# Expert gate and up weights each as one 4 MB transfer, and the token rows turned by half-identity products

## The reference

```python
lg_exp = ((x2 @ w_re) + b_re).reshape(N, N_GROUPS, EXPERTS_PER_GROUP)     # N = 384 tokens
lg_in = lg_exp[jnp.arange(N), g_sel[:, 0]]
top_v, top_i = lax.top_k(lg_in, TOP_K)                                    # 2 of 8 experts
...
def expert_block(args):                                                   # 32 experts
    xblk, e = args
    return (jax.nn.silu(xblk @ w_eg[e]) * (xblk @ w_eu[e])) @ w_ed[e]     # 2048 -> 512 -> 2048
...
return jax.ops.segment_sum(yb.reshape(n_slots, D) * slot_w[:, None], slot_tok, num_segments=N)
```

## Time and profile before

| | |
|---|---|
| median of three runs | 1981.06 us (1980.61 to 1982.42) |
| the profiled execution | 1982.1 us, of which the span of its instructions is 1980.5 us |
| mean granted TensorE clock | 0.913 of full speed |
| PE busy / PEld busy | 82% / 42% of the span |
| DMA queue of SP | 559.14 MB, 69.5% of 16 engines' span |
| DMA queue of GpSimd | 36.16 MB, 5.4% |

### The profile page before, as it was taken

One profiled execution on the slowest core, in us unless ns is written; L12 is line 12 of the kernel. 1 busy time (PEld: TensorE's weight loads), 2 busy tenths in 40 slices (PEclk: granted clock), 3 DMA queues, 4 the chain that ended last, 5 costly groups with the idle time before them and its releaser, 6 DMA issues.

```text
span 1980.5 us, 21568 instructions
## 1 busy us (share of the span) xinstructions
PE 1622.2 (82%) x8889; PEld 839.3 (42%) x8889; DVE 390.9 (20%) x848; ACT 207.1 (10%) x511; POOL 166.9 (8%) x342
## 2 busy tenths in 40 slices
PE   6899999999986699985888887787878878878850
PEld 2455554444434244444544443444434444444420
DVE  2011212214415100134111111011011110111106
ACT  3001111111122000011000000000000000000003
POOL 1300000000120100002010110110101101001002
PEclk9999999999989799955888989999999889999885
DMA  9986665655560433071799999999999999999953
GB/s 366 338 293 260 229 261 221 261 219 213 212 203 12 170 106 106 31 305 24 319 424 426 428 427 427 427 427 427 425 420 427 423 423 426 424 425 420 422 231 134
DMA packets 100002, 602.26 MB, mean 304 GB/s; under 512 B 15349, under 2 KB 17509, under 8 KB 64745
## 3 DMA queue, kind: packets, MB, share of 16 engines
q1 hardware_dynamic: 83810, 559.14, 69.5%
q0 software_dynamic: 15328, 36.16, 5.4%
q10 hardware_dynamic: 816, 6.29, 0.8%
HBM read 594.65 MB, written 28.10 MB: 314 GB/s over the span
## 4 chain that ended last, share of the span: by engine, by line
PE 47%; DMA 43%; DVE 5%; issue 2%; ACT 1%; POOL 1%; SPq 0%; POOLq 0%; DVEq 0%; ACTq 0%
DMA ring<-in_w_expert_up 35%; PE bank L790 9%; PE bank L1071 8%; PE bank L1153 7%; PE bank L786 6%; DMA zbuf<-h_rows,cur 3%; PE bank L743 3%; PE bank L1174 3%; PE bank L730 2%; DMA ring<-in_w_ada 2%; PE bank L709 1%; PE bank L734 1%; DMA xbuf<-in_x_sample 1%; DMA h_rows<-zbuf 1%; DMA ring<-in_w_in 1%
## 5 line engine op out<-in xcount | busy, mean ns | idle before, releaser
L1153 PE MATMUL bank<-ring,zbuf 128*64 128x256 f32 x4096 | 465.8, 384 | 84.2 <-DMA ring<-in_w_expert_up 75.6
L1153 PEld LDWEIGHTS bank<-ring,zbuf 128*64 128x64 f32 x4096 | 292.6, 138 | 265.3 <-DMA ring<-in_w_expert_up 96.7
L1174 PE MATMUL bank<-ring,hbuf 128*64 128x512 f32 x1024 | 265.7, 678 | 17.4 <-ACT hbuf L1428 17.4
L790 PE MATMUL bank<-ring,hbuf 128*128 128x512 f32 x384 | 173.3, 601 | 0.4 <-ACT xbuf L1256 0.2
L1174 PEld LDWEIGHTS bank<-ring,hbuf 128*64 128x64 f32 x1024 | 81.5, 156 | 182.1 <-issue 180.5
L786 PE MATMUL bank<-hbuf,ring 128*128 128x384 f32 x384 | 129.9, 492 | 1.2 <-DVE zbuf L1572 1.2
L1893 DVE TENSOR_SCALAR hbuf<-hbuf 128x256 f32<-128x256 f32 x32 | 9.4, 294 | 534.6 <-ACT hbuf L1420 534.6
L790 PEld LDWEIGHTS bank<-ring,hbuf 128*128 128x128 f32 x384 | 70.3, 190 | 92.3 <-issue 91.8
L786 PEld LDWEIGHTS bank<-hbuf,ring 128*128 128x128 f32 x384 | 71.0, 190 | 57.9 <-issue 13.4
L1136 PE MATMUL bank<-ident,zbuf 128*128 128x128 f32 x264 | 43.4, 314 | 58.0 <-DMA zbuf<-h_rows,cur 58.0
L1071 PE MATMUL bank<-ring,zbuf 128*128 128x512 f32 x192 | 85.7, 607 | 4.2 <-DVEq L1773 4.2
(11 more groups left out here) (371 smaller groups left out, 1205.3 us busy)
## 6 DMA issues: line engine op xcount, KB each, us to landing
ring<-in_w_expert_gate SPq DMA_DIRECT2D x64, 2048.0 KB, 25.3
ring<-in_w_expert_up SPq DMA_DIRECT2D x64, 2048.0 KB, 26.6
ring<-in_w_expert_down SPq DMA_DIRECT2D x64, 2048.0 KB, 23.7
ring<-in_w_ada SPq DMA_DIRECT2D x96, 1024.0 KB, 8.8
ring<-in_w_in SPq DMA_DIRECT2D x32, 1024.0 KB, 8.5
ring<-in_w_out SPq DMA_DIRECT2D x16, 1024.0 KB, 5.0
ring<-y_rows ACTq DMA_DIRECT2D x3, 2048.0 KB, 12.0
h_rows<-zbuf POOLq DMA_DIRECT2D x3, 1024.0 KB, 11.4
```

Source lines behind the costliest of these rows:

```text
L790: last = mm(bank[t][:, :], hT[:, k, t * P:(t + 1) * P], w[:, kk_, :], start=(k == 0), stop=(k == KC - 1))
L1153: last = mm(bank[2 + u][64 * q:64 * q + 64, 256 * (j // 4):256 * (j // 4) + 256], xeT[u][:, k % 8, k // 8, :], w[:, kk_, 256 * q:256 * q + ...
L1174: last = mm(bank[5 + n][64 * q:64 * q + 64, :], hidT[u][:, k % 2, k // 2, :], unit(8 + k)[:, 1024 * q + QN * n:1024 * q + QN * n + QN], st ...
```

## The change

The gate and the up matrix of an expert are each fetched by one transfer of 4 MB into four units (`unit_quad`), with 16 neighbouring rows, 32 KB in one piece, for a partition; the down matrix stays two transfers of 2 MB in 16 KB pieces. SP issues four transfers for an expert in place of six, waits for all four units to be read before each of the large ones, and TensorE waits for the whole 4 MB before it reads the first of their units.

As partition p now holds rows 16p to 16p + 15, the turned token rows must be laid out alike: value 16p + k of a token on partition p. In `rows_T` the stationary block is then `xg` with a stride of 16 floats (64 columns), and the product with one half of the identity matrix picks the first or second half of the tokens' values: 32 products of 128x64 by 64 columns in place of 8 transposes of 128x128. Copies and `up` keep their sizes.

```diff
+        def unit_quad(s):
+            return ring[:, s * D:(s + 4) * D]
+
+        EXPERT_LOADS = ((0, 4), (4, 4), (8, 2), (10, 2))
+
+        def expert_rows_of(e, j):
+
+            if j < 8:
+                return unit_quad(j), (eg_v, eu_v)[j // 4][:, bass.ds(e, 1), :].rearrange("p e f -> p (e f)")
+            return unit_pair(j), ed_v[:, bass.ds(e, 1), (j - 8) // 2, :].rearrange("p e f -> p (e f)")
...
-        xeT = [zbuf[:, 2048 + 1024 * u:3072 + 1024 * u].rearrange("p (c q s) -> p c q s", c=8, q=2)
+        xeT = [zbuf[:, 2048 + 1024 * u:3072 + 1024 * u].rearrange("p (k s) -> p k s", k=KC)
...
-        eg_v = A["w_expert_gate"][0].rearrange("e (g p c) f -> p e g (c f)", g=2, c=8)
-        eu_v = A["w_expert_up"][0].rearrange("e (g p c) f -> p e g (c f)", g=2, c=8)
+        eg_v = A["w_expert_gate"][0].rearrange("e (p c) f -> p e (c f)", c=16)
+        eu_v = A["w_expert_up"][0].rearrange("e (p c) f -> p e (c f)", c=16)
...
-                for j in range(0, UE, 2):
+                for j, n in EXPERT_LOADS:
                     if first:
-
-
-                        if j < 4:
-                            last = max(n for n in range(U_MOE) if w_slot(n) in (j, j + 1))
-                            sp.wait_ge(unit_used, last + 1)
+                        if j == 0:
+                            sp.wait_ge(unit_used, U_MOE)
...
                     else:
-                        sp.wait_ge(unit_used, U_MOE + UE * (e - 1) + j + 2)
-                    half_v = (eg_v, eu_v, ed_v)[j // 4][:, bass.ds(e, 1), j % 4 // 2, :]
-                    sp.dma_start(unit_pair(j), half_v.rearrange("p e f -> p (e f)")).then_inc(loaded[j], 16)
+                        sp.wait_ge(unit_used, U_MOE + UE * (e - 1) + j + n)
+                    dst, src = expert_rows_of(e, j)
+                    sp.dma_start(dst, src).then_inc(loaded[j], 16)
...
-                rows = xg[u].rearrange("p (n c) -> p c n", c=8)
-                for c in range(8):
-                    last = tr(bank[c // 4][:, (c % 4) * P:(c % 4 + 1) * P], rows[:, c, :], ident[:, :])
+                rows = xg[u].rearrange("p (n k) -> p k n", k=KC)
+                for k in range(KC):
+                    for q in range(2):
+                        r = slice(64 * q, 64 * q + 64)
+                        last = mm(bank[k // 8][r, (k % 8) * W:(k % 8 + 1) * W], rows[:, k, :], ident[:, r], start=True, stop=True)
                 last.then_inc(eT_ps, 1)
 
             def expert_landed(j, e):
-                j -= j % 2
+                j -= j % (4 if j < 8 else 2)
...
-                                      xeT[u][:, k % 8, k // 8, :], w[:, kk_, 256 * q:256 * q + 256],
+                                      xeT[u][:, k, :], w[:, kk_, 256 * q:256 * q + 256],
```

More of the change, by code:

```diff
@@ L425, in _ @@
                     e = sp.value_load(ov_i[0:1, bass.ds(i + 1, 1)], min_val=0, max_val=NE - 1)
[L426 to L429, removed]
+                    for j, n in EXPERT_LOADS:
+                        sp.wait_ge(unit_used, U_MOE + UE * (NE - 1) + UE * i + j + n)
+                        dst, src = expert_rows_of(e, j)
+                        sp.dma_start(dst, src).then_inc(loaded[j], 16)
             with sp.Else():
@@ L1415, in rows_copy @@
                 act.wait_ge(eT_ps, n + 1)
-                cp(xeT[u][:, 4:8, :, :].rearrange("p c q s -> p (c q s)"), bank[1][:, :]).then_inc(eT_a, 1)
+                cp(xeT[u][:, 8:16, :].rearrange("p k s -> p (k s)"), bank[1][:, :]).then_inc(eT_a, 1)
             def exp_gate(u, e):
@@ L1887, in rows_copy @@
                 dve.wait_ge(eT_ps, n + 1)
-                cp(xeT[u][:, 0:4, :, :].rearrange("p c q s -> p (c q s)"), bank[0][:, :]).then_inc(eT_v, 1)
+                cp(xeT[u][:, 0:8, :].rearrange("p k s -> p (k s)"), bank[0][:, :]).then_inc(eT_v, 1)
             def hidden(u, e):
```

## The result

The changed kernel takes 2020.5 us (median of four runs, 2012.0 to 2026.2) against 1980.8 us: a ratio of 1.0193, with a 95% interval from 1.0161 to 1.0225. The forecast was 2026, slower. The profiled execution has a span of 2018.6 us against 1980.5, 38.1 us more.

What follows compares the result with a forecast made beforehand. The byte stream (30.4 us per expert) was the bound, the gather loop (29.0) just under it. Late-gather intervals of 37.1 us alternating with 26.6 average 31.85; times 31, that adds 45.4 us: 2026 us, range 1984 to 2095.

Steps and rivals of the forecast that it cites:

- What bounds the kernel: Expert stage: the byte stream sets its length, 30.4 to 30.7 us per expert, with the gather loop close at 29.0 us.
- Part 1: Gathers beside the weight stream: turns double with 32 KB pieces, 0 to +11 us a gather, taken as +6.6.
- mixture: Gather's surroundings: 60% beside gate and up pieces, the rest beside down weights or an empty queue.
- Part 2: `rows_T`: 32 products for 8 take 3.0 us, +1.5 us (ends +0.7 and +3), counting where the gather is late.
- Part 3: Waits on four units: stream starts 3.4 us later, last `up` ends 3.67 us later; hidden in the forecast time.
- Part 4: Gate and up in fewer, larger pieces: 0 to 4.6 us less, counting only where the byte stream is the limit.
- The sum: Expert intervals: long 37.1 and short 26.6 us in turn, mean 31.85, times 31, +45.4 us; chance 0.66.
- R1: Rival: small transfers held up no longer than now, the stream stays the bound, +2.5 to +7 us, 1986; chance 0.20.
- R2: Rival: the weight stream gains by transfer size, at most 4.6 us of pieces, 1976.5 us; chance 0.03.
- the Trainium skill's 2.0 us fixed per transfer: Weight loads: 64 transfers fewer would save 128 us, giving 1853; the prediction held that the trace disagrees.
- R3: Rival: every expert interval is long as the weight queue never runs dry, +208 us, 2189; chance 0.08.
- The signs: Expected profile: gathers over 20 and 8 to 14 us, half late by 5 to 10, DMA share under 0.97, reload near 955.

Runs made afterwards that it cites:

- e2: The changed kernel with gate and up again in 2 MB pairs of 16 KB pieces, leaving only the new `rows_T`: 1988.7 us, ratio 1.0026 to the kernel before.
- e4: The kernel before with every gather issued one expert earlier: 1984.7 us, ratio 1.0005 to the kernel before.
- e1: The kernel before with gate and up each one 4 MB transfer, waits on four units, 16 KB pieces, old `rows_T`: 1989.5 us, ratio 1.0025.
- e5: The kernel before with all expert weights in 1 MB transfers, pieces of 8 KB: 1995.6 us, ratio 1.0061 to the kernel before.
- e3: The changed kernel with every gather issued one expert earlier: 1985.5 us, ratio 0.9999 to the kernel before.
- e9: The changed kernel, gathers one expert earlier, expert 1's gate in four 1 MB transfers, last expert's up in two of 2 MB: 1977.8 us, ratio 0.9961.

## Why the prediction was right, step by step

- **What bounds the kernel** held. Two loops of nearly equal length, 29.0 against 30.4 us: e2 made the gather late in 31 cases with some 2 us more, e4 gained nothing without the gather in the path.
- **Part 1, pieces and turns**: the mechanism held, and a piece is one packet. The size was too large. Doubling a piece adds at most 16 x 0.61 = 9.8 us, not 11 (by the one-for-one order that holds at 8 and 16 KB). And the mixture was not 60% beside large pieces: the late gathers take 17.7 us on average (22 of them between 14.7 and 20.2 us; besides there are the first two, eight of under 9 us and a last one of 12.4), 3.5 over 14.2, which is 36%. They are issued close behind the end of `down`, when down weights are still in the queue. The short ones land in 6.6 to 8.8 us, below the 8 to 14 that I gave, because the queue beside them was empty for a time.
- **Part 2, `rows_T`**: too small. I counted 32 products, as the code has, but a float32 product is two instructions in the trace and a transpose one: the earlier trace rows show 8 instructions for 8 transposes, and 128 for the 64 products of `up` (where the description of the kernel says 128 and 32 products, it counts instructions). The row of the changed kernel, after a wait:

```profile
1130.16 3.94 PE L1146 MATMUL bank<-ident,zbuf 128*64 128x64 f32 x64 [7.72 <-DMA zbuf<-h_rows,cur]
```

  64 instructions take 3.94 us, 2.0 more than the 1.97 to 1.99 of a late one before, inside the ends of +0.7 and +3. Alone, in e2, it cost 0.26%, 5 us, within the 1981 to 2000 expected there.
- **Part 3, the waits on four units**: +5 us in e1 against 7.1 reckoned, which lies at the upper end of its interval (3 to 7). That the term is hidden in the changed kernel, as said, fits the sum of the intervals below but was not tested by a run of its own.
- **Part 4, fewer pieces**: it didn't count in the changed kernel, as forecast, since the stream is not its bound. Fixed cost of a piece: e5 has 1536 pieces more per engine and takes 12 us more, 8 ns each (192 more transfers are in it) against the 9 ns of the earlier trace rows. From 16 to 32 KB the stream gains 425 to 426 GB/s, which is too coarse to price a piece. The lower end of 0, taken from 430 GB/s at 1926 us, was a misreading: a window of 4 us of a short burst doesn't measure a rate to 1%.
- **The sum**: 31.85 us per interval forecast, 31.55 measured, but from two errors that offset each other. The long intervals were to be 37.1 us and the short ones 26.6, in turn. Measured, from the ends of `down` in the timeline: 8 short ones of 25.5 and 23 others of 33.65 on average, (8 x 25.5 + 23 x 33.65) / 31 = 31.55. The short interval was right in its terms (`up` 13.99, way to `down` 4.6, `down` 7.09 in place of 8.0). The long one was forecast 3.5 us too long, by part 1; and being only 3 us over the stream's 30.5 and not 6.6, two or three of them pass before the stream runs into the full ring and a short one comes. That 2026 lies so close to 2020.5 is therefore partly luck. The order of long and short should follow from the lag between stream and gather. Runs of the changed kernel differ by 14 us, and those of the kernel before by 2 us beside them (by 7 and 9 us in the two largest sets of the experiments); whether that order is the reason was not looked into.
- **The rivals**: R1 (small transfers not held up) fell on the landing times, R2 (the stream gains by size) on 426 GB/s, and the Trainium skill's 2.0 us fixed per transfer (DMA: Bandwidth & Descriptors, Anatomy of one DMA) on the same row: with transfers queued ahead, 64 fewer of them gave back none of the 128 us. The page has the figure under the path of GpSimd, for one transfer; the weights are issued by SP. R3 (always long) fell because the stream does stop.
- **The signs**: right were gathers of two kinds, waits of 7.2 us on average (165.6 us in 23 waits, without the first) and the holes in the stream. The first reload came at 958.6 us, not near 955, but `up` itself had begun 3.9 us later; counted from there it is 3.2 us later than before, for 3.4 forecast. Off in size were the long gathers (17.7 us, and not 20 and more), the share of late ones (24 of 33, and not half), `rows_T` (3.7 to 4.0 us for 3) and the DMA share, 0.98 from 1100 to 1880 us where it was to be under 0.97.

Left open: the 2.0 us by which the first `down` ends later in the changed kernel's profile. The start of the expert stage lies between 945.5 and 952.3 us in the profiles of these kernels, also in those that change nothing ahead of it.

## What to carry to other kernels

When a small transfer shares the DMA engines with a saturated stream, each of its rows waits for a piece of the stream, so enlarging the pieces is paid by every gather and scatter beside it; look for the slack of the loop that waits for them (here 1.5 us in 30) before making pieces larger. If a gather is on the path, issue it a step earlier: its buffer is free from the moment its last contents are read, and the waits ahead of it in its queue may have nothing to do with it. Coarser waits cost little in a stage with a deep ring (5 us of 1981 in e1, nothing to be told between e3 and e4); what there is to gain lies at the two ends, and splitting the first and the last large transfer gave some 8 us (e9).

## What the runs showed of the hardware that I had not expected

- A row of a gather costs one piece of the weight stream, 0.31 us at 8 KB and 0.61 us at 16 KB, and so does a row of an empty place (from 1311.5 to 1313.5 us of the kernel before, 60 such packets with 0.00 MB went beside 60 of the weight queue). The constant stays: 5.4 to 5.5 us with the gather alone, 4.4 behind a scatter, against 3.4 us for a gather on idle engines. Beside a mixture of 16 and 32 KB pieces the gather alone takes 15.1 us (10.3 beside 16 KB).
- The order is one packet of one queue, one of the other (264 and 262 packets in 10 us), also where a transfer has 16 pieces for an engine (261 and 260).
- A scatter pays as well: it lands after 7.9 us beside 8 KB pieces, 10.3 beside 16 KB and 12.6 beside the mixture (e5, before, e3).
- 8 KB pieces run at 419 GB/s, 16 KB at 425 and 16 with 32 KB at 426: hardly anything is gained over 16 KB.
- A float32 product of 64 by 64 columns costs 2 instructions of 58 ns each (3.72 us for 64, without a wait), a 128x128 transpose one (1.16 us for 8): the same data turned by products took 3.2 times as long.
